# A hybrid decoder layer in one launch: the output projection by seven half products for two tiles, in one block with the gates, and the first expert weights requested later

## The chip, the core and the metric

The kernel is one program on one core of a Trainium2 chip. The metric is the device time of one execution in microseconds. All matmuls are float32 and each appears in the trace as two matmul records, so that a count of records is twice the count of matmuls in the code.

## What is computed

One inference step of one decoder layer, for 512 prompt tokens and 32 new tokens (8 sequences of 4), which travel together as 544 columns. The parts that matter here are the end of the mixer and the mixture of experts:

```
merged = g_a * (y_a @ w_out_ssm) + g_b * (y_b @ w_out_att) + g_c * (y_c @ w_out_sc)   # gates: sigmoid
x = x + gate1 * (merged @ w_o)                      # w_o: 1024 x 1024, the output projection
h = rms_norm(x, norm2_w) * (1 + scale2) + shift2
x = x + gate2 * hier_moe(h)                         # 32 experts, two for each token
# hier_moe: router logits, top group, top 2 in it, then for each expert
# silu(h @ w_gate[e]) * (h @ w_up[e]) @ w_down[e]   # 1024 x 256, 1024 x 256, 256 x 1024
```

## The kernel before, in words

The activations lie transposed: 128 partitions, 8 chunks of features, 544 columns, and `HALF` is 272 columns. A weight tile is 128 output features by 1024 input features (512 KB). SP loads such tiles in one long order into a ring of 8 buffers. Semaphore `w_used` counts the tiles that TensorE has finished with, and the load of tile n waits for it to reach n - 7.

**The gates (end of the block that begins before L1460).** Eight steps, w = 0 to 7, each take two weight tiles. Put as a 2 x 2 block product (two output tiles, two halves of the input features, two halves of the columns) a pair of tiles is eight products of four matmuls each (`half_product`, L362), and the kernel makes it with seven: VectorE forms four sums of weight halves (`weight_sum`, L383) and four sums of activation blocks (`act_sums`), and puts the seven results together from PSUM (`block_step`, L388 to L401). Results wait in 8 PSUM banks in turn. After each second step VectorE multiplies by the gate and adds into `merged` (L2024, L2025).

**The output projection (a block of its own, L2120 to L2149 and on).** A block starts when all five engines have met at a barrier. TensorE takes the eight tiles of `w_o`, numbers `T_O` to `T_O` + 7, one after the other with `project` (L350): 16 matmuls of 128 x 128 by 272 columns for a tile. VectorE adds each tile, times gate1, to `xT` (L2145 to L2148) and counts `s_res`. SP loads `xT` again at the block's start (L2123). ScalarE squares and scales each finished chunk of x, GpSimd adds the squares, and TensorE begins the router's logits (L2204) when seven chunks are done.

**The experts (same block).** The 32 experts are handled as 16 pairs. For each pair SP loads the gate and up weights (two DMAs of 2048 KB, L2366, three buffers) and the down weights come in two DMAs of 1024 KB (pairs 0 and 1 from SP at L2371, the others from ScalarE's queue at L2503, two buffers). The rows of h are written to DRAM (`h2_rows`, from ScalarE's queue, L2189), and GpSimd gathers the rows of a pair from there with an indirect DMA (L2403) and scatters the results (L2411). TensorE turns the gathered rows (L2426), makes gate and up (L2440), then the down product of the pair before (L2461). What orders SP's queue is written out by hand:

```
with sp.Fori(0, trips) as r:
    gate_up_in(r, 0)
    down_in(r, 0)
    down_in(r, 1)
    sp.wait_ge(w_used, T_END)
    gate_up_in(r, 1)
    sp.wait_ge(s_slot, 1)
    ...
    sp.wait_ge(gath[0], r * (8 * NP) + 16)
    for p in range(2, NP):
        gate_up_in(r, p)
```

So pairs 0 and 1 are requested before the first gathered rows have landed, and pair 2 only after they have. Pair 3 waits until the gate and up product of pair 0 has freed its buffer, and so on.

## Time and profile before

| | |
|---|---|
| median of 3 runs | 1494.41 us (1492.55 to 1501.58) |
| the profiled execution, its own time | 1493.89 us |
| its span in the trace | 1492.2 us |
| TensorE busy | 1357.6 us, 91% of the span |
| VectorE, ScalarE, GpSimd busy | 44%, 17%, 9% |
| output projection, first to last matmul | 1111.9 to 1173.6 us |
| first expert matmuls to the end of the last pair | 1198.6 to 1448 us |
| read from HBM over the span | 234.47 MB |

The span is the stretch that the trace covers; 1.7 us of the execution's own time lie around it. The shares are means over stages with different limits, so that the stages are read one by one below. "PEclk" is the clock that TensorE was granted as a share of 2.4 GHz, and 0.50 is its lower level, 1.2 GHz.

### The profile page before, as it was taken

To read this page: it belongs to the slowest core of one execution; us is meant where nothing else is said; L and a number is where in the kernel's file an instruction comes from. 1 tells how busy PE (TensorE), PEld (TensorE's weight loads), DVE (VectorE), ACT (ScalarE), POOL (GpSimd) and SP (SyncE) were. 2 spreads that over 40 slices of the span, in tenths; PEclk is the share of its full clock that TensorE was granted. 3 is DMA by queue.
4 is the path that set the end of the run, shared out by engine and by line. 5 is a ranking of instruction groups with operands and counts; after the bars stand their busy time and mean duration, and the time that the engine had idled before them with its cause. 6 is when DMAs were issued, how large, how long until landed. Compare 5 with 4: busy or idle time off the path is not lost. (4 is left out here: it accounts for less than half of the span.)

```text
span 1492.2 us, 19377 instructions
## 1 busy us (share of the span) xinstructions
PE 1357.6 (91%) x7089; PEld 977.8 (66%) x7089; DVE 662.2 (44%) x1371; ACT 257.7 (17%) x554; POOL 139.5 (9%) x270
## 2 busy tenths in 40 slices
PE   4999999999999999899989988899989888878784
PEld 2787677878778788576767766688878633222233
DVE  1635677555667756110115557575541412111125
ACT  2201211221223521110112122310001300000001
POOL 0223000000000000122210002000001111111111
PEclk9999999999999999899999997999999989999995
DMA  8463323322322223556461102321245489999945
GB/s 343 166 135 107 101 63 113 124 84 91 113 85 91 99 77 111 167 163 205 163 237 43 43 29 88 143 63 65 85 151 220 173 340 425 425 424 425 409 157 180
DMA packets 62208, 250.87 MB, mean 168 GB/s; under 512 B 10058, under 2 KB 20714, under 8 KB 53002
## 3 DMA queue, kind: packets, MB, share of 16 engines
q1 hardware_dynamic: 42130, 185.31, 34.0%
q10 hardware_dynamic: 10264, 44.97, 8.4%
q0 software_dynamic: 9728, 19.42, 3.9%
q8 instruction: 57, 0.93, 0.3%
q14 instruction: 29, 0.24, 0.1%
HBM read 234.47 MB, written 22.91 MB: 172 GB/s over the span
## 5 line engine op out<-in xcount | busy, mean ns | idle before, releaser
L350 PE MATMUL psum<-arena 128*128 128x272 f32 x2048 | 488.2, 397 | 10.4 <-DVE arena L1997 4.8
L350 PEld LDWEIGHTS psum<-arena 128*128 128x128 f32 x2048 | 391.2, 192 | 103.3 <-issue 16.3
L362 PE MATMUL psum<-arena 128*128 128x272 f32 x840 | 197.3, 394 | 0.0
L362 PEld LDWEIGHTS psum<-arena 128*128 128x128 f32 x840 | 157.6, 189 | 39.8 <-issue 6.7
L1203 PE MATMUL psum<-arena 128*128 128x272 f32 x512 | 124.4, 401 | 0.0
L2440 PE MATMUL psum<-arena 128*64 128x512 f32 x512 | 115.2, 601 | 2.7 <-DVE arena L2539 2.7
L1203 PEld LDWEIGHTS psum<-arena 128*128 128x128 f32 x512 | 97.3, 193 | 26.1 <-DVE arena L1334 4.1
L2440 PEld LDWEIGHTS psum<-arena 128*64 128x64 f32 x512 | 35.8, 136 | 70.9 <-issue 70.9
L2461 PE MATMUL psum<-arena 128*64 128x512 f32 x256 | 69.3, 690 | 1.2 <-DVE arena L2528 1.2
L1334 DVE TENSOR_TENSOR arena<-arena,psum 128x272 f32<-128x272 f32 x16 | 7.0, 439 | 140.2 <-ACT arena L1286 140.2
L1522 PE MATMUL psum<-arena 128*128 128x272 f32 x256 | 64.7, 407 | 2.9 <-PEq L206 2.9
L1039 DVE MATCH_REPLACE8 arena<-arena 32x1056 f32<-32x1056 f32 (+3 forms) x80 | 64.9, 817 | 0.0
L1036 DVE MAX8 arena<-arena 32x8 f32<-32x1056 f32 (+3 forms) x80 | 63.4, 825 | 0.9 <-DVE arena L727 0.3
L1017 DVE SCALAR_TENSOR_TENSOR arena<-psum,arena 128x128 f32<-128x128 f32 (+3 forms) x32 | 15.7, 491 | 99.8 <-PE psum L840 99.8
L1522 PEld LDWEIGHTS psum<-arena 128*128 128x128 f32 x256 | 49.8, 199 | 13.7 <-issue 3.1
L2426 PE MATMUL psum<-arena 128*128 128x128 f32 x128 | 22.5, 333 | 37.2 <-DMA arena<-h_rows,arena 37.1
L2520 DVE TENSOR_TENSOR arena<-arena,psum 128x256 f32<-128x256 f32 x16 | 6.8, 422 | 108.0 <-ACT arena L2509 108.0
L2426 PEld LDWEIGHTS psum<-arena 128*128 128x128 f32 x128 | 17.6, 169 | 50.3 <-DMA arena<-h_rows,arena 45.7
L2461 PEld LDWEIGHTS psum<-arena 128*64 128x64 f32 x256 | 19.8, 158 | 40.9 <-issue 39.5
L572 POOL DMA_DIRECT2D arena<-in_pages_i x64 | 33.3, 521 | 118.5 <-issue 112.2
L2528 DVE TENSOR_SCALAR arena<-psum,arena 128x1024 f32<-128x1024 f32 x16 | 20.6, 1284 | 51.1 <-PE psum L2461 51.1
L335 PE MATMUL psum<-arena 128*32 128x512 f32 x192 | 24.8, 636 | 19.9 <-DMA arena<-in_weights 19.9
(374 smaller groups left out, 1414.9 us busy)
## 6 DMA issues: line engine op xcount, KB each, us to landing
arena<-in_weights SPq DMA_DIRECT2D x153, 512.0 KB, 4.4
arena<-in_w_gu SPq DMA_DIRECT2D x32, 2048.0 KB, 17.5
arena<-in_w_down ACTq DMA_DIRECT2D x28, 1024.0 KB, 17.1
arena<-in_weights ACTq DMA_DIRECT2D x16, 512.0 KB, 4.2
arena<-in_x SPq DMA_DIRECT2D x2, 2176.0 KB, 10.7
arena<-in_pages_k POOLq DMA_DIRECT2D x32, 128.0 KB, 3.2
arena<-in_pages_k SPq DMA_DIRECT2D x32, 128.0 KB, 2.6
arena<-in_pages_v SPq DMA_DIRECT2D x32, 128.0 KB, 2.9
```

The source lines that it names most:

```text
L335: mm = pe.matmul(psum[32 * j:32 * j + 32, bank, :], lhsT=c_silu[:, 2 * j + c2, :], rhs=ring[:, (first + j) % RING, c2 * 512:c2 * 512 + 512 ...
L350: mm = pe.matmul(out[:, h, :], lhsT=w_of(n, c), rhs=act[:, c, h * HALF:(h + 1) * HALF], start=(c == 0), stop=(c == DC - 1))
L362: mm = pe.matmul(out, lhsT=w[:, c * P:c * P + P], rhs=x[:, c, :], start=(c == 0), stop=(c == 3))
L572: pool.dma_start(kidx[64 * a:64 * a + 64, bass.ds(b, 1), j * PAGE:(j + 1) * PAGE].rearrange("p a n -> p (a n)"), ins["pages_i"][bass.ds(of ...
L1036: dve.max(best8[0:s.shape[0], i, :], s).then_inc(s_top, 1)
L1039: dve.match_replace(s, best8[0:s.shape[0], i, :], s, CHOSEN).then_inc(s_top, 1)
L1203: mm = pe.matmul(psum[:, bank, 0:HALF], lhsT=w_of(n, c), rhs=act_of[:, c, h * HALF:(h + 1) * HALF], start=(c == 0), stop=(c == DC - 1))
L1522: mm = pe.matmul(psum[:, (2, 7)[k % 2], 0:HALF], lhsT=w_of(n, c), rhs=act_of[:, c, (k % 2) * HALF:(k % 2 + 1) * HALF], start=(c == 0), sto ...
L2426: mm = pe.transpose(psum[:, c // 4, (c % 4) * P:(c % 4) * P + P], xg[:, p % 2, c * P:c * P + P], const("ident"))
L2440: mm = pe.matmul(psum[CAP * e:CAP * e + CAP, 2 + k, :].rearrange("p (o f) -> p o f", o=2), lhsT=xgT[:, k, at:at + CAP], rhs=wv[:, c], star ...
L2461: mm = pe.matmul(psum[CAP * e:CAP * e + CAP, 4 + h, :], lhsT=actT[:, k, at:at + CAP], rhs=w_dn[k][:, e, f * D + h * 512:f * D + h * 512 + ...
L2528: dve.tensor_scalar(yst[:, k, :].rearrange("p (a n) -> p a n", n=512), psum[:, 4:6, :], wtab[:, p:p + 1], None, ALU.mult).then_inc(s_yo, 1)
```

## The change

The projection is made like the gates: two tiles at a time (v = 0 to 3), seven half products each. It stands in the gates' block now, with no barrier between. The halves of a pair's two tiles are taken in swapped order (`SWAPPED`), so that the tile with the lower number is finished first, at step k = 5, and the other at k = 6. The weight sums of a pair are formed during the pair before, those of v = 0 in the gates' last step. The sums of the activations, `t_m`, lie where the first expert buffer `a_q` is, so SP requests no expert weights before `s_res` has reached 8; and `s_gu`, which the first request waits for too, is raised by TensorE only at `T_END`.

```diff
+        SWAPPED = (1, 0)
+        t_m = [A.at(a_q + 4 * HALF * i, 4, HALF) for i in range(4)]
...
-                        if w + 1 < N_SEVEN:
-                            weight_sum(dve, n + 2, wsum[:, (w + 1) % 2], k, sum_link)
+                        weight_sum(dve, n + 2, wsum[:, (w + 1) % 2], k, sum_link, SWAPPED if w + 1 == N_SEVEN else (0, 1))
...
+                    dve.wait_ge(s_mgw, w // 2 + 1)
+                    if w == 3:
+                        act_link(dve.tensor_tensor(t_m[0], block_of(merged, 0, 1), block_of(merged, 0, 0), ALU.subtract))
...
-        with nc.Block() as block:
             @block.sync
             def _(sp):
                 sp.dma_start(xT, ins["x"]).then_inc(s_x10, 16)
 
             @block.tensor
             def _(pe):
-                pe.sem_inc(s_gu, 2)
-                pe.sem_inc(s_dn, 2)
-                for u in range(8):
-                    tile_ready(pe, T_O + u)
-                    if u >= 4:
-                        pe.wait_ge(s_res, u - 3)
-                    project(pe, T_O + u, pair[u % 4], merged).then_inc(w_used, 1)
+                for v in range(4):
+                    n = T_O + 2 * v
+                    for k, (wv, x) in enumerate(seven_operands(n, sums_o[v], merged, t_m, SWAPPED)):
+                        j = 7 * v + k
+                        if k == 0:
+                            tile_ready(pe, n + 1)
+                            pe.wait_ge(s_mgw, 2)
+                        if j == 1:
+                            pe.wait_ge(s_mgw, 4)
+                        if k == 2:
+                            pe.wait_ge(s_wsum, 4 * (N_SEVEN + v) + 2)
+                            pe.wait_ge(s_asum, 10)
+                        if k == 3:
+                            pe.wait_ge(s_wsum, 4 * (N_SEVEN + v) + 3)
+                            pe.wait_ge(s_asum, 11)
+                        if k == 4:
+                            tile_ready(pe, n)
+                            pe.wait_ge(s_asum, 12)
+                        if k == 6:
+                            pe.wait_ge(s_wsum, 4 * (N_SEVEN + v) + 4)
+                        pe.wait_ge(s_took, 53 + j if j < 4 else max(56, 49 + j))
+                        mm = half_product(pe, psum[:, (j + 4) % 8, 0:HALF], wv, x)
...
+                    if v == 1:
+                        pe.wait_ge(w_used, T_O + 2)
+                        pe.sem_inc(s_dn, 2)
+                pe.wait_ge(w_used, T_END)
+                pe.sem_inc(s_gu, 2)
...
+                def residual(m, src):
+                    gate, dst, new = mods[:, 16 + m, :], xT[:, m, 0:SEQ], xT[:, m, SEQ:NT]
+                    dve.scalar_tensor_tensor(dst, src[:, 0:SEQ], gate[:, 0:1], dst, ALU.mult, ALU.add)
...
+                        block_step(dve, k, psum[:, (7 * v + k + 4) % 8, 0:HALF], (part8[:, 0, :], part8[:, 1, :]),
+                                   blocks_of(tmw), took)
+                        for i in {2: (0, 1), 3: (2,), 5: (3,)}.get(k, ()):
+                            if v < 3:
+                                weight_sum(dve, n + 2, sums_o[v + 1], i, sum_link, SWAPPED)
+                        if k >= 5:
+                            if v == 0 and k == 5:
+                                dve.wait_ge(s_x10, 16)
+                            residual(2 * v + k - 5, tmw[:, 6 - k, :])
...
                 with sp.Fori(0, trips) as r:
+                    sp.wait_ge(s_res, DC)
                     gate_up_in(r, 0)
                     down_in(r, 0)
```

What this does to the order of instructions is shown at three places. The names of waits there are those under which a semaphore was first allocated; many are used again under other names.

TensorE before, from the last half product of the gates into the projection's first two tiles (L1460 and L2125 are the end and the start of the blocks; `qk_ready` stands for the weight sums):

```order
L362 MATMUL psum<-arena 128x272 [waits dve_link3,qk_ready]
L362 MATMUL psum<-arena 128x272 x3
L1460 UNCONDITIONAL_BRANCH
L2125 UNCONDITIONAL_BRANCH [waits barrier_Pool_Activation_PE_DVE_SP_release]
L350 MATMUL psum<-arena 128x272 [waits w_full1]
L350 MATMUL psum<-arena 128x272 x15
L350 MATMUL psum<-arena 128x272 [waits w_full2]
L350 MATMUL psum<-arena 128x272 x15
```

The same place now (`exp_ready` is `s_mgw`, the merged tiles; `logits_read` is `s_asum`, the sums of activations; `dve_link3` is `s_took`):

```order
L362 MATMUL psum<-arena 128x272 [waits dve_link3,qk_ready]
L362 MATMUL psum<-arena 128x272 x3
L2132 UNCONDITIONAL_BRANCH
L362 MATMUL psum<-arena 128x272 [waits dve_link3,exp_ready,w_full2]
L362 MATMUL psum<-arena 128x272 x3
L362 MATMUL psum<-arena 128x272 [waits dve_link3,exp_ready]
L362 MATMUL psum<-arena 128x272 x3
L362 MATMUL psum<-arena 128x272 [waits dve_link3,logits_read,qk_ready]
L362 MATMUL psum<-arena 128x272 x3
L362 MATMUL psum<-arena 128x272 [waits dve_link3,logits_read,qk_ready]
L362 MATMUL psum<-arena 128x272 x3
```

The barrier is gone from between the two stages, and two tiles take 7 x 4 matmuls where they took 2 x 16.

VectorE before, the last tile of the projection (L2145 waits for TensorE's last matmul of it):

```order
L2145 SCALAR_TENSOR_TENSOR arena<-psum,arena 128x272 [waits rel_in_dram,w_used]
L2145 SCALAR_TENSOR_TENSOR arena<-psum,arena 128x240
L2146 TENSOR_TENSOR arena<-psum,arena 128x32
L2148 TENSOR_TENSOR arena<-arena 128x32 [waits rel_in_dram]
L2150 TENSOR_SCALAR arena<-arena 128x512 [waits rel_in_dram]
```

VectorE now, from the sixth product of the last pair to the same L2150 (L2198 now); `top_step` counts the half products:

```order
L398 TENSOR_TENSOR arena<-arena,psum 128x272 [waits top_step,dve_link3]
L399 TENSOR_TENSOR arena<-arena,psum 128x272
L2173 SCALAR_TENSOR_TENSOR arena<-arena 128x512 [waits dve_link3]
L2174 TENSOR_TENSOR arena<-arena 128x32
L2175 TENSOR_TENSOR arena<-arena 128x32 [waits rel_in_dram]
L401 TENSOR_TENSOR arena<-arena,psum 128x272 [waits rel_in_dram,w_used]
L2173 SCALAR_TENSOR_TENSOR arena<-arena 128x512 [waits dve_link3]
L2174 TENSOR_TENSOR arena<-arena 128x32
L2175 TENSOR_TENSOR arena<-arena 128x32 [waits rel_in_dram]
L2198 TENSOR_SCALAR arena<-arena 128x512 [waits rel_in_dram]
```

Chunk 6 is finished between the last two products, and one step of the seven stands ahead of chunk 7.

SP before, from the last ring load to the last request ahead of pair 2:

```order
L308 DMA arena<-in_weights 128x1024 [waits w_used]
L1460 UNCONDITIONAL_BRANCH
L2121 UNCONDITIONAL_BRANCH [waits barrier_Pool_Activation_PE_DVE_SP_release]
L2123 DMA arena<-in_x 128x4352
...
L2366 DMA arena<-in_w_gu 128x4096 [waits sturned_out]
L2366 DMA arena<-in_w_gu 128x4096
...
L2371 DMA arena<-in_w_down 128x2048 [waits short_in_psum]
...
L2366 DMA arena<-in_w_gu 128x4096 [waits sturned_out,w_used]
L2366 DMA arena<-in_w_gu 128x4096
```

SP now (`modulation_turned` is `s_res`):

```order
L308 DMA arena<-in_weights 128x1024 [waits w_used]
L2128 UNCONDITIONAL_BRANCH
L2130 DMA arena<-in_x 128x4352
...
L2414 ISA [waits modulation_turned]
L2416 DMA arena<-in_w_gu 128x4096 [waits satt_out]
L2416 DMA arena<-in_w_gu 128x4096
...
L2421 DMA arena<-in_w_down 128x2048 [waits short_gate]
...
L2416 DMA arena<-in_w_gu 128x4096 [waits satt_out,w_used]
L2416 DMA arena<-in_w_gu 128x4096
```

The order of SP's queue is the same; the load of x has lost the barrier ahead of it, and the first request of expert weights has gained the wait for all eight residuals.

## Rows read from the trace of the kernel before

**Rows 1.** Windows: us, busy time by engine (records), PEclk, DMA share, GB/s.

```profile
1173.50:1190.00 16.50, 13.54 (x128) 9.64 (x127) 11.48 (x67) 6.91 (x9) 1.35 (x2) 1.00 0.94 360
1190.00:1198.50 8.50, 4.33 (x80) 3.94 (x80) 2.90 (x18) 3.03 (x5) 2.13 (x2) 0.62 0.39 120
1198.50:1230.00 31.50, 28.74 (x130) 11.84 (x132) 5.80 (x6) 1.54 (x4) 4.03 (x4) 0.89 0.94 374
1230.00:1400.00 170.00, 137.40 (x600) 49.65 (x596) 29.74 (x31) 8.07 (x21) 20.18 (x20) 0.91 1.01 424
```

**Rows 2.** Waits from 1190 us on: who for whom, total us, times, longest.

```profile
PE psum L2426 <- DMA arena<-h_rows,arena: 37.1, 12, 4.4
```

**Rows 3.** Timeline from the last gates to the projection: start, us, engine, line.

```profile
1085.68 22.23 PE L362 MATMUL psum<-arena 128*128 128x272 f32 x96
...
1094.13 0.69 DVE L383 TENSOR_TENSOR arena<-arena 128x512 f32<-128x512 f32 x1
...
1108.01 0.44 DVE L401 TENSOR_TENSOR arena<-arena,psum 128x272 f32<-128x272 f32 x1 [1.05 <-PE psum L362]
1108.48 1.29 DVE L2024 TENSOR_TENSOR arena<-arena 128x1088 f32<-128x1088 f32 x1
...
1109.81 1.29 DVE L2025 TENSOR_TENSOR arena<-arena 128x1088 f32<-128x1088 f32 x1
1111.59 0.35 SPq L2123 DMA_DIRECT2D arena<-in_x  x1
...
1111.94 61.63 PE L350 MATMUL psum<-arena 128*128 128x272 f32 x256 [4.03 <-PEq L1460]
```

**Rows 4.** Windows of the projection's first 8 us, columns as above.

```profile
1112.00:1116.00 4.00, 4.00 (x9) 3.07 (x10) 0.00 (x0) 1.09 (x2) 1.66 (x1) 0.50 0.97 311
1116.00:1120.00 4.00, 4.00 (x17) 3.20 (x17) 0.00 (x0) 0.00 (x0) 0.00 (x0) 0.89 1.03 443
```

**Rows 5.** Timeline: VectorE takes tiles 1 and 2 of the projection.

```profile
1129.39 0.88 DVE L2145 SCALAR_TENSOR_TENSOR arena<-psum,arena 128x272 f32<-128x272 f32 x2 [6.10 <-PE psum L350]
...
1136.76 0.88 DVE L2145 SCALAR_TENSOR_TENSOR arena<-psum,arena 128x272 f32<-128x272 f32 x2 [6.17 <-PE psum L350]
```

**Rows 6.** Timeline at the end of the projection.

```profile
1173.50 3.22 PE L2204 MATMUL psum<-arena 128*36 128x256 f32 x28
1173.60 25.70 SPq L2366 DMA_DIRECT2D arena<-in_w_gu  x4
1173.61 0.88 DVE L2145 SCALAR_TENSOR_TENSOR arena<-psum,arena 128x272 f32<-128x272 f32 x2 [6.17 <-PE psum L350]
...
1174.61 0.19 DVE L2148 TENSOR_TENSOR arena<-arena 128x32 f32<-128x32 f32 x1
```

**Rows 7.** DMA requests from 1112 to 1132 us: count, size of each, us to landing.

```profile
arena<-in_w_gu SPq DMA_DIRECT2D x2, 2048.0 KB, 15.4
arena<-in_w_down SPq DMA_DIRECT2D x4, 1024.0 KB, 22.5
```

**Rows 8.** DMA requests from 1173 to 1198 us, columns as above.

```profile
h_rows<-arena ACTq DMA_DIRECT2D x4, 512.0 KB, 6.5
h_rows<-arena ACTq DMA_DIRECT2D x1, 128.0 KB, 2.9
arena<-h_rows,arena POOLq DMA_INDIRECT x2, 3.9
```

**Rows 9.** Landing of L2123's load of x (all of the run).

```profile
DMA to landing us min/median/max: 8.8/8.8/8.8
```

**Rows 10.** Landing of L2403's third gather, requested at 1201.37.

```profile
DMA to landing us min/median/max: 11.3/11.3/11.3
```

**Rows 11.** Timeline of the experts: the first gather, and TensorE after two waits.

```profile
1194.36 1.12 POOL L2403 DMA_INDIRECT arena<-h_rows,arena  x1 [12.48 <-issue]
...
1248.45 1.97 PE L2426 MATMUL psum<-arena 128*128 128x128 f32 x8 [3.93 <-DMA arena<-h_rows,arena]
...
1415.24 1.09 PE L2426 MATMUL psum<-arena 128*128 128x128 f32 x8 [2.43 <-DMA arena<-h_rows,arena]
```

More of the change, by code:

```diff
@@ L369, in act_sums, with tile_halves, weight_sum @@
                 link(dve.tensor_tensor(out, a, b, ALU.subtract))
-        def tile_halves(n):
-            return [ring[:, (n + i) % RING, 512 * k:512 * k + 512] for i in range(2) for k in range(2)]
-        def weight_sum(dve, n, sums, k, link):
-            a11, a12, a21, a22 = tile_halves(n)
+        def tile_halves(n, order=(0, 1)):
+            return [ring[:, (n + i) % RING, 512 * k:512 * k + 512] for i in order for k in range(2)]
+        def weight_sum(dve, n, sums, k, link, order=(0, 1)):
+            a11, a12, a21, a22 = tile_halves(n, order)
             if k == 0:
@@ new lines, in build @@
+            s_h2w = [sem(f"h2_written{i}") for i in range(4)]
+            acc11 = A.at(a_e + 2048, NT)
+            sq11 = A.at(a_e + 2048 + NT, 4, NT)
+            a_r11 = a_w + 8 * D
+            std11 = A.at(a_r11, P)
+            std_new = A.at(a_r11 + P, NEW)
+            lgT = A.at(a_r11 + 160, 256)
+            lgT_new = A.at(a_r11 + 416, NEW, parts=36)
+            rcol = A.at(a_r11 + 448, 5)
+            dshift = A.at(a_r11 + 456, DC, NB)
+            a_r = a_r11 + NT
+            NR = 5
@@ new lines, in build @@
+            W_LG = NE + 8
+            lg = A.at(a_r, NR, W_LG)
+            g8, e8 = A.at(a_r + 220, NR, 8), A.at(a_r + 260, NR, 8)
+            gi8, ei8 = A.at(a_r + 300, NR, 8), A.at(a_r + 340, NR, 8)
+            gif, eif = A.at(a_r + 380, NR, 1), A.at(a_r + 385, NR, 2)
+            goh = A.at(a_r + 395, NR, NG)
+            gexp = A.at(a_r + 415, NR, NG)
+            gsum = A.at(a_r + 435, NR)
+            masked = A.at(a_r + 440, NR, NE)
+            pen = A.at(a_r + 600, NR, NG)
+            full = [A.at(a_r + 720 + 160 * k, NR, NE) for k in range(2)]
@@ new lines, in build @@
+            wcol = A.at(a_param + PARAM_AT["conv_prev"][0], 2, NR)
+            a_keep = a_param + PARAM_AT["conv_prev"][0] + 16
+            rounds_i = A.at(a_keep + 20, 1).bitcast(I32)
+            rows11 = A.at(a_xb + DC * NT - 2 * D, 4, D)
+            assert T_O % RING + 3 < RING and T_END - T_O == RING
+            sums_o = [wsum[:, 0], A.at(a_xb + DC * NT, 4, 512)] + [
+                A.at(a_ring + (T_O + 2 * v) % RING * 1024, 4, 512) for v in range(2)]
+            h2_rows = nc.dram_tensor("h2_rows", [NT, D], F32).ap()
@@ L2148, in _ @@
                     link(dve.tensor_tensor(new, new, tmp, ALU.add))
                     dve.sem_inc(s_res, 1)
+                for out, a, b in ((t_m[1], block_of(merged, 1, 1), t_m[0]),
+                                  (t_m[2], block_of(merged, 1, 1), block_of(merged, 0, 1)),
+                                  (t_m[3], block_of(merged, 1, 0), t_m[1])):
+                    act_link(dve.tensor_tensor(out, a, b, ALU.subtract))
+                for v in range(4):
+                    n = T_O + 2 * v
+                    for k in range(7):
+                        if k < 6:
+                            dve.wait_ge(s_prod, 6 * (N_SEVEN + v) + k + 1)
+                        else:
+                            dve.wait_ge(w_used, n + 2)
+                        block_step(dve, k, psum[:, (7 * v + k + 4) % 8, 0:HALF], (part8[:, 0, :], part8[:, 1, :]),
[7 more added lines that the diff above has]
+                            residual(2 * v + k - 5, tmw[:, 6 - k, :])
```

169 lines of the change are left out of this document (70 added, 99 removed).

## The prediction

> **What bounds the kernel now.** I read the windows of busy time first, since they tell which resource is full in which stage. In the projection TensorE never pauses once it has begun: 61.63 us for 256 matmul records [rows 3]. In the router and the row writing no single resource is full, and a chain through all engines sets the time; the DMA engines move 360 GB/s in its first part and 120 in its last 8.5 us [rows 1]. From 1230 to 1400 us the DMA share is 1.01 at 424 GB/s while TensorE works 137 of 170 us [rows 1]: the experts run at the speed of the weight stream. The list of waits says the same from TensorE's side: it waits 12 times, 37.1 us in all, for gathered rows [rows 2], which travel in that full stream. The last of these waits ends at 1415.24 [rows 11]; from there TensorE works from pair to pair. So the reader should keep two clocks apart: when TensorE is done with the projection, and when the DMA engines have moved what the gather behind 1415.24 has ahead of it. All times below are in the profiled execution (span 1492.2, own time 1493.89, 0.5 under the median of the runs).
>
> **The projection, part by part.**
>
> Matmuls: 96 records of half products took 22.23 us, eight records to a product, so 12 products, 1.85 us each [rows 3]. Four tile pairs take 28 products where they took 32: 4 x 1.85 = 7.4 us less.
>
> The barrier: TensorE ended the gates at 1107.91 and began the projection at 1111.94, 4.03 us later [rows 3]. Now product 0 needs only merged tiles 0 to 3, long ready, and runs at once, to 1109.8. Product 1 needs `merged` complete: VectorE's L401, L2024 and L2025 end at 1109.81 + 1.29 = 1111.1 [rows 3]. I take 1111.2, so 1.4 us of idleness are left and 2.6 us go. Behind it the sums t_m[1] to t_m[3] cost 1.29 each, like L2025; they are ready by 1112.5, 1113.8 and 1115.1, and products 2, 3 and 4 want them at 1113.0, 1114.9 and 1116.7. The margin is 0.5 us at the narrowest.
>
> The clock: after the 4.03 us of idleness TensorE was granted 0.50 (1.2 GHz) for the next 4 us and 0.89 on average in the 4 after [rows 4]. A tile at full clock took 1136.76 - 1129.39 = 7.37 us [rows 5], eight would be 59.0, and 61.63 were spent: 2.7 us of loss. An idle time of 2.43 us was followed by eight records in 1.09 us, one of 3.93 us by the same eight in 1.97 us [rows 11], so I take it that 1.4 us leave the clock at its upper level. Bounds: 0 and 2.7 us.
>
> TensorE then ends at 1111.2 + 27 x 1.85 = 1161.2 instead of 1173.57 [rows 3], 12.4 us earlier.
>
> What hides the rest: VectorE has in 7 x 1.85 = 13.0 us eight steps of 0.44 (L401), four weight sums of 0.69 (L383) [rows 3] and two residuals of about 1.1, together 8.5 us. Without that cover each us of excess would be paid four times. The load of x, 8.8 us from request to landing [rows 9], is now requested once the products of the gates are done, some 2.5 us before the 1111.59 of today [rows 3]; it lands by 1118 and is wanted after product 5, at 1120.4.
>
> The tail: today the eighth residual is done 1.2 us after TensorE (1174.8 against 1173.57) [rows 6]. Now the sixth product's two steps (0.8) and residual 6 (about 1.1) fill VectorE to about TensorE's end + 0.1, then one step (0.44) and residual 7 (1.1): done at + 1.7, or 1162.9. TensorE's first logits want the seventh residual, at + 0.2 instead of at once (L2204) [rows 6], and those of the last chunks have the whole row of 28 matmul records ahead of them: 0.3 us of the gain goes back. The router would thus be 12 us early.
>
> **The weights, part by part.** Before, pairs 0 and 1's down weights and pair 0's gate and up weights came during the projection: 2 x 2048 + 4 x 1024 KB = 8.4 MB [rows 7], when the DMA engines had nothing else. Only pair 1's gate and up followed at 1173.60 [rows 6]. Now all four sets, 12.6 MB, start at 1162.9. At 424 GB/s the 8.4 MB that are moved cost 19.8 us of a resource that is full later. Three stretches have room for them, each read as its length x (1 - rate / 424) [rows 1]: 16.5 us at 360 give 2.5, 8.5 us at 120 give 6.1, 31.5 us at 374 give 3.7. Together 12.3 us.
>
> The stream ended its critical part at 1415.2, 241.6 us after the request at 1173.60. The same now: 1162.9 + 241.6 - 12.3 + 19.8 = 1412.0, if every gap is filled. Two will not be: about 1 us from a request to its first bytes, and about 1 us where pair 3 must wait for pair 0's gate and up product (both are estimates; the gaps themselves are inside the 12.3). That makes 1414.0 and a change of **-1.2 us**. The bounds of this term are -3.2 us (all gaps filled) and the case below in which the gaps come back.
>
> The sum needs the first gather to land before the queue of weights runs dry, since pair 2 is requested only then. Queue and row writes hold 12.6 + 2.2 MB = 35 us, to about 1198.8. The gather was requested 20.8 us after TensorE's end (1194.36) [rows 11]. With 0.3 us of tail, and the last row write slower than its 2.9 us [rows 8] by some 2.5 us (the large ones took 6.5 beside a weight load [rows 8]), that is 1184.8. A gather beside a weight load took 11.3 us [rows 10], against 3.9 in a quiet stretch [rows 8]: landing at 1196.1, before the queue is dry, and 2 to 3 us before today's 1198.5. After 1415 nothing changes.
>
> A rule of the Trainium skill speaks to the last step. The third gather, requested into a running weight load, took 11.3 us, but had to wait until about that load's end [rows 10]; this alone doesn't tell whether it was served side by side or after. "DMA: Bandwidth & Descriptors", under Queues, rings and completion order, says that each of the 16 engines goes round between its queues packet by packet. By that rule the gather is served side by side at any depth of the queue, and the sum is the one above; without it, it would be the second rival's.
>
> **Rivals.**
>
> *The lead arrives whole.* If the experts were paced by the gather's delay and not by bytes, everything would shift by 12.4 - 0.3 = 12.1 us: 1481.8. For it: TensorE waits for rows and not for weights [rows 2]. Against it: the DMA share of 1.01 for 170 us [rows 1]; a delay with free bandwidth would show less. Half of it could still come through if the 424 GB/s can be exceeded a little. Chance 0.08.
>
> *The gather starves, and it ends slower.* If rows are served only when the weights queued ahead are done, the first gather lands as much after the dry queue as the third did after its load: two transfers, 4.2 MB or 9.9 us, requested at 1198.5 and under way 1 us later, end at 1209.4; the gather landed at 1201.37 + 11.3 = 1212.7 [rows 10], 3.3 us after. So it lands at 1198.8 + 3.3 = 1202.1 where it landed at 1198.5. Nothing overlaps, pair 2 is requested 3.6 us late, and the time is 1497.5. It decides from the point where the landing is later than 1198.5, that is, when the gather takes over 14 us. Slower row writes ahead of it could add some 3 us. For it: gathers deep in the stream take much longer than 11.3. Against it: those compete with two queues more. Chance 0.22.
>
> *The clock stays down after the 1.4 us.* TensorE ends 2.7 us later, every request too: +1.5 us, 1495.4. Chance 0.1.
>
> *The half products don't do what they say:* if a sum or a bank came late once in each pair of tiles, by 1 to 2 us, the lead would shrink by 4 to 8 us, and through the stream's start all of it would show: 1497 to 1501. The margin of 0.5 us above is the only thin one and occurs once, so 0.05.
>
> **How the numbers follow.** My forecast, 0.55, is -1.2 us: **1492.7 us**, with its own range from 1490.5 to 1495. The range of 8 in 10 reaches to the starving gather above, 1499, and part of the way to the whole lead below, 1486. A measurement of this kernel can't tell a change under about 1% (15 us) from none. None of the cases leaves that band; what does must be something that I don't see. Slower gets a little more, 0.06, since a bubble in the stream would repeat with each pair; faster 0.03; within 1% 0.91.
>
> **What would show it.** In the profile of the changed kernel: one idle time of 1.4 us on TensorE before the second projection product, at full clock after it; 28 products in about 52 us, ending near 1161; the eighth residual near 1163, with the weight requests right behind it; the DMA share full from there through the router, where it now sinks to 0.39; the first gather taking 8 to 14 us, landing near 1196; the last wait of TensorE for rows ending at about 1414. The prediction is wrong if the DMA share shows holes before 1230, if the gather lands after 1200, or if the experts' stretch from first to last matmul shrinks below today's.

## The result, and the profile after

Before, the median of 20 runs was 1496.92 us; after, also of 20, it was 1503.76 us (1498.65 to 1507.88). The ratio is 1.0047, with a 95% interval of 1.0036 to 1.0058: 7.0 us slower (5.4 to 8.7), where 1.2 us faster was forecast with a range that ended at 1499. One of the 20 runs before took 3171.76 us, twice as long as the others, and the ratio leaves it out.

The profiled execution (span 1505.2, own time 1506.99) has 6.4 of its extra microseconds before the change begins: the gates' last product ends at 1114.35 instead of 1107.91, with the same instructions ahead of it. The other kernels below, with that same code ahead, reach this point between 1107.3 and 1111.1, so I take this part for scatter from run to run; the medians of the 20 runs bear this out, as they differ by 6.8 us and not by the 13 of the two spans. I therefore count all times from two marks: **G**, the end of the gates' last product, and **E**, the end of TensorE's work for the projection. The third mark, **D**, is the start of the last down product (16 records of 128x512).

The timeline of the changed kernel around the projection and the router (start, us, engine and line, operation, tiles, count, then idle time before it and who ended it), with the first row write, and then where the experts begin and end:

```profile
1116.24 1.29 DVE L2026 TENSOR_TENSOR arena<-arena 128x1088 f32<-128x1088 f32 x1
1117.59 49.91 PE L362 MATMUL psum<-arena 128*128 128x272 f32 x216 [1.42 <-DVE arena L2026]
...
1117.78 3.95 DVE L2181 TENSOR_TENSOR arena<-arena 128x1088 f32<-128x1088 f32 x3 [0.25 <-DVE arena L2026]
...
1167.80 3.22 PE L2253 MATMUL psum<-arena 128*36 128x256 f32 x28 [0.30 <-DVEq L2176]
...
1170.70 0.82 SPq L2416 DMA_DIRECT2D arena<-in_w_gu  x2
...
1171.65 2.06 SPq L2421 DMA_DIRECT2D arena<-in_w_down  x4
...
1173.82 0.93 SPq L2416 DMA_DIRECT2D arena<-in_w_gu  x2
...
1176.45 0.34 ACTq L2238 DMA_DIRECT2D h_rows<-arena  x1
...
1186.37 1.01 ACT L2236 ACTIVATE arena<-psum 32x1024 f32<-32x1024 f32 x1 [5.35 <-DMA h_rows<-arena]
1187.41 0.34 ACTq L2238 DMA_DIRECT2D h_rows<-arena  x1
...
1200.03 1.12 POOL L2454 DMA_INDIRECT arena<-h_rows,arena  x1 [23.85 <-issue]
...
1210.40 0.82 SPq L2416 DMA_DIRECT2D arena<-in_w_gu  x2
1210.51 1.97 PE L2477 MATMUL psum<-arena 128*128 128x128 f32 x8 [17.07 <-DMA arena<-h_rows,arena]
...
1457.68 3.65 PE L2512 MATMUL psum<-arena 128*64 128x512 f32 x16 [1.20 <-DVE arena L2579]
```

The first row write, the first turning and D in the kernel before:

```profile
1182.14 0.34 ACTq L2189 DMA_DIRECT2D h_rows<-arena  x1
...
1198.59 1.97 PE L2426 MATMUL psum<-arena 128*128 128x128 f32 x8 [2.06 <-DMA arena<-h_rows,arena]
...
1444.46 3.65 PE L2461 MATMUL psum<-arena 128*64 128x512 f32 x16 [1.20 <-DVE arena L2528]
```

The first half is what the change promised. The 4.03 us in front of the projection [rows 3] have become 1.42; 216 records in 49.91 us follow without a pause; E is 1117.59 + 49.91 = 1167.50. From G that is 53.15 us, against 65.66 before: TensorE has a lead of **12.5 us**. The lead is gone when TensorE turns its first gathered rows. Before, that was at 1198.59, 25.0 us after E. Now it is at 1210.51, 43.0 us after E: 18.0 us more. 18.0 - 12.5 = 5.5 us late, and D - G has grown by 6.8 us (1457.68 - 1114.35 = 343.3; before 1444.46 - 1107.91 = 336.6). TensorE's wait for the rows was 17.07 us long, where it had been 2.06.

Why the rows are late stands in the DMA requests from 1160 to 1210 us (count, size of each, median us to landing), to be held against [rows 8]:

```profile
h_rows<-arena ACTq DMA_DIRECT2D x4, 512.0 KB, 13.3
h_rows<-arena ACTq DMA_DIRECT2D x1, 128.0 KB, 11.4
arena<-h_rows,arena POOLq DMA_INDIRECT x2, 10.4
```

The gather took 10.4 us; 11.3 had been forecast. But it was requested 32.5 us after E instead of 20.8, as it waits for all five row writes. The four large ones took 13.3 us instead of 6.5 in the median, and the small last one 11.4 instead of 2.9. ScalarE had to wait 5.35 us for the first write before it could prepare the last. How the two streams share the DMA engines is seen in the queues' packets (packets, MB, share): in the changed kernel from 1190 to 1195, with q1 carrying weights and q10 the row writes,

```profile
q1 hardware_dynamic: 197, 1.39, 66.3%
q10 hardware_dynamic: 196, 0.74, 36.0%
```

and in the kernel before from 1187 to 1191, when the weights of pair 1 are in and only rows are left:

```profile
q10 hardware_dynamic: 430, 1.55, 94.7%
q1 hardware_dynamic: 1, 0.00, 0.0%
```

One packet of the one, one of the other: beside weights the row writes get 0.74 MB in 5 us, or 150 GB/s, and alone 390. This is the rule of the Trainium skill that the prediction weighed ("DMA: Bandwidth & Descriptors", Queues, rings and completion order: each engine goes round between its queues packet by packet), and the trace agrees. I had applied it to the gather and not to the writes ahead of it.

The windows after (us, busy time by engine with records, PEclk, DMA share, GB/s) answer to [rows 1]:

```profile
1178.00:1203.00 25.00, 9.41 (x108) 8.06 (x108) 8.09 (x44) 6.13 (x7) 2.13 (x2) 0.63 1.01 419
1203.00:1211.00 8.00, 0.49 (x3) 0.49 (x4) 0.00 (x0) 0.00 (x0) 0.00 (x0) 0.50 0.77 323
1211.00:1230.00 19.00, 16.33 (x69) 6.89 (x70) 2.87 (x3) 0.77 (x2) 2.00 (x2) 0.80 0.90 346
1230.00:1400.00 170.00, 140.49 (x616) 50.72 (x613) 30.96 (x32) 8.07 (x21) 20.20 (x20) 0.91 1.01 423
```

The router's stretch is full now (1.01), as forecast. But the queue runs dry before the gather lands (the DMA share is 0.97 from 1206 to 1209 and 0.17 from 1209 to 1211), and the gap comes back as 0.77 and 0.90 until pair 2, requested at 1210.40, fills it.

### The profile page after: what moved, and what is told of

Read it like the earlier page. It is cut to its first block and busy times, and to the rows that moved or that the text cites. A ratio compares the mean times of both kernels' runs of the same rounds, so it can differ in the third digit from the quotient of the medians.

```text
span 1505.2 us, 19389 instructions
## 1 busy us (share of the span) xinstructions
PE 1355.8 (90%) x7057; PEld 976.3 (65%) x7057; DVE 695.8 (46%) x1415; ACT 257.7 (17%) x554; POOL 141.8 (9%) x270
## 5 line engine op out<-in xcount | busy, mean ns | idle before, releaser
L350 PE MATMUL psum<-arena 128*128 128x272 f32 x1792 | 426.3, 396 | 5.8 <-DVE arena L1998 4.8
L350 PEld LDWEIGHTS psum<-arena 128*128 128x128 f32 x1792 | 340.9, 191 | 87.0 <-issue 11.9
L362 PE MATMUL psum<-arena 128*128 128x272 f32 x1064 | 249.1, 393 | 1.4 <-DVE arena L2026 1.4
L362 PEld LDWEIGHTS psum<-arena 128*128 128x128 f32 x1064 | 199.9, 189 | 50.6 <-issue 6.7
L1203 PE MATMUL psum<-arena 128*128 128x272 f32 x512 | 125.3, 403 | 0.0
L1203 PEld LDWEIGHTS psum<-arena 128*128 128x128 f32 x512 | 98.0, 194 | 26.7 <-DVE arena L1334 4.1
L1524 PE MATMUL psum<-arena 128*128 128x272 f32 x256 | 64.8, 407 | 2.9 <-PEq L206 2.9
L1039 DVE MATCH_REPLACE8 arena<-arena 32x1056 f32<-32x1056 f32 (+3 forms) x80 | 64.9, 817 | 0.0
L2477 PEld LDWEIGHTS psum<-arena 128*128 128x128 f32 x128 | 17.4, 168 | 65.8 <-DMA arena<-h_rows,arena 46.2
L1524 PEld LDWEIGHTS psum<-arena 128*128 128x128 f32 x256 | 49.8, 199 | 13.6 <-issue 3.1
L383 DVE TENSOR_TENSOR arena<-arena 128x512 f32<-128x512 f32 x76 | 52.7, 693 | 2.6
L2590 DVE TENSOR_TENSOR arena<-psum,arena 128x1024 f32<-128x1024 f32 x16 | 19.6, 1225 | 61.9 <-PE psum L2477 61.9
L2512 PEld LDWEIGHTS psum<-arena 128*64 128x64 f32 x256 | 19.8, 159 | 41.2 <-issue 39.8
## 6 DMA issues: line engine op xcount, KB each, us to landing
arena<-in_x SPq DMA_DIRECT2D x2, 2176.0 KB, 11.7
```

The lines of the kernel that those rows point to most:

```text
L350: mm = pe.matmul(out[:, h, :], lhsT=w_of(n, c), rhs=act[:, c, h * HALF:(h + 1) * HALF], start=(c == 0), stop=(c == DC - 1))
L362: mm = pe.matmul(out, lhsT=w[:, c * P:c * P + P], rhs=x[:, c, :], start=(c == 0), stop=(c == 3))
L383: link(dve.tensor_tensor(sums[:, k], a, b, op))
L1039: dve.match_replace(s, best8[0:s.shape[0], i, :], s, CHOSEN).then_inc(s_top, 1)
L1203: mm = pe.matmul(psum[:, bank, 0:HALF], lhsT=w_of(n, c), rhs=act_of[:, c, h * HALF:(h + 1) * HALF], start=(c == 0), stop=(c == DC - 1))
L1524: mm = pe.matmul(psum[:, (2, 7)[k % 2], 0:HALF], lhsT=w_of(n, c), rhs=act_of[:, c, (k % 2) * HALF:(k % 2 + 1) * HALF], start=(c == 0), sto ...
```

## The experiments

Two explanations were tested. **The writes** (theory 1, "turns", in what was expected of the runs): the late request for weights makes the row writes slow, so the gather is late, and everything behind the first turning follows it at a fixed distance. **The bytes** (theory 2): 8.4 MB moved out of an idle stretch cost their time in a full one, whatever the gather does. Below each run is told with D - G against the 336.6 us of before, which is free of the scatter ahead of G.

**before_late.** The old projection with only the weights asked for later.

```diff
                 with sp.Fori(0, trips) as r:
+                    sp.wait_ge(s_res, DC)
                     gate_up_in(r, 0)
```

> The kernel before, with one line more: SP waits for all eight residuals before the first request of expert weights; projection, barrier and all else as before. E is the end of TensorE's last projection matmul; in the kernel before the first gathered rows land at E + 24.9 and TensorE's last wait for rows ends at E + 241.7, in the changed one at E + 42.9 and E + 260.8. Theory 1 (turns): the DMA engines take the queues in turn, packet by packet, so the row writes crawl as long as weights are queued; the first gather's landing comes late, and the end follows it by 217 us. Then this kernel shows the delay alone: landing near E + 41, last wait near E + 258.5, +17 us against before. Theory 2 (bytes): only the 8.4 MB that now fall into the busy stretch count, less the gaps that they fill: +9.5 us, landing near E + 33.

Measured: ratio 1.0091 (1.0070 to 1.0113), +13.6 us. D - G is 353.4, or +16.8. The timeline shows the same crawl without the new projection:

```profile
1204.72 1.12 POOL L2404 DMA_INDIRECT arena<-h_rows,arena  x1 [23.55 <-issue]
...
1214.26 1.97 PE L2427 MATMUL psum<-arena 128*128 128x128 f32 x8 [16.77 <-DMA arena<-h_rows,arena]
```

The large writes took 12.3 us, the last one 12.0, and the first turning came 41.4 us after E. The +16.8 and the landing are those of the writes; the bytes alone would have given +9.5, which lies below the interval of the ratio (10.5 to 16.9 us). So the late request alone costs 14 us, and the new projection beside it gives back 13.6 - 7.0 = 6.6 us (10.0 by D - G).

**down_first.** The change, but with the down weights of pairs 0 and 1 asked for as early as before. Of the 8.4 MB, only pair 0's gate and up weights (4.2 MB) stay late.

```diff
                 with sp.Fori(0, trips) as r:
-                    sp.wait_ge(s_res, DC)
-                    gate_up_in(r, 0)
                     down_in(r, 0)
                     down_in(r, 1)
+                    sp.wait_ge(s_res, DC)
+                    gate_up_in(r, 0)
```

> The changed kernel with SP's first requests in another order: the down weights of pairs 0 and 1 (4.2 MB) as soon as the first pair of projection tiles is done, only then the wait for the eight residuals and the gate and up weights of pairs 0 and 1. Theory 1 (turns): behind 8.4 MB instead of 12.6 the weights run dry at about E + 26, the row writes end at about E + 28, the first gather lands at about E + 32.5 instead of E + 42.9, and the end moves by the same 10 us: 10 us faster than the changed kernel, 3 to 4 faster than before. Theory 2 (bytes): 4.2 MB less in the full stretch is worth 9.9 us only if the gaps stay filled; the landing moves little. A third, that the hole in the DMA share after 1205 us is what costs: the hole stays, since pair 2 is still requested at the landing, and the gain is under 5 us.

Measured: 0.9996 (0.9978 to 1.0013). The first turning is 37.6 us after E, D - G +2.3. I had expected the writes to be freed sooner and the rows to land near E + 32.5: the large ones took 16.6 us, longer than in the change. The queues from 1174 to 1179 show why:

```profile
q1 hardware_dynamic: 119, 1.69, 79.1%
q10 hardware_dynamic: 117, 0.44, 21.4%
```

Again one packet for one. But a packet of weights here has 1.69 MB / 119 = 14 KB in the mean, where it had 7 KB in the changed kernel from 1190 to 1195, and a packet of rows 3.8 KB. The sizes stand in the packet records: gate and up weights travel in packets of 16384 bytes, down weights in 8192 and rows in 4096, each the run of one partition, with some of 4 bytes between them that lower the means. So the writes get 88 GB/s: what a small transfer gets beside a large one depended here on the packets of the large one.

**quiet.** The change with no expert weights at all until the first gather has landed.

```diff
                 with sp.Fori(0, trips) as r:
+                    sp.wait_ge(gath[0], r * (8 * NP) + 16)
                     sp.wait_ge(s_res, DC)
```

> The changed kernel with no expert weights requested at all until the first gathered rows have landed, so that the row writes and the first gather run with nothing beside them. Theory 1 (turns): the row writes take about 3 us each instead of 9.8 to 16.5, the last one under 3 instead of 11.4, the gather about 3.9; landing at E + 23 to E + 25, as the router's chain alone allows. All 12.6 MB and pair 2 then come after it: 29.7 us of stream where 9.9 stood before, so the last wait is near E + 24 + 217 + 18 = E + 259, about the same as the changed kernel (within 4 us). Theory 2 (bytes): the router's chain and the landing hardly depend on the weights (over E + 35), and the end is 15 us later than the changed kernel's.

Measured: 1.0131 (1.0107 to 1.0156), +19.6 us; D - G +17.6. The writes took 2.6 and 2.0 us, and the first turning came 25.8 us after E, 17 us sooner than in the change. Then TensorE stands for weights:

```profile
1188.32 1.96 PE L2478 MATMUL psum<-arena 128*128 128x128 f32 x8 [1.45 <-DMA arena<-h_rows,arena]
...
1202.33 9.37 PE L2492 MATMUL psum<-arena 128*64 128x512 f32 x32 [12.05 <-DMA arena<-in_w_gu]
...
1223.01 9.27 PE L2492 MATMUL psum<-arena 128*64 128x512 f32 x32 [9.92 <-DMA arena<-in_w_gu]
```

This shows both: without weights beside them the writes are fast, and the bytes are a cost of their own once the rows are early. My forecast of its end was too low: I had counted 18 us of stream still to come behind the rows, and the stretch from the first turning to D grew by 28 us over the changed kernel's (275.3 against 247.2). For this kernel's time the bytes account, 15 us over the changed kernel, was the nearer one (12.6 by the ratios).

**split_writes.** The change with the second and fourth row write issued by GpSimd, so that the writes stand in two queues and should get two turns of three.

```diff
+                    if i in (1, 3):
+                        return
                     act.wait_ge(s_row_sb, i + 1)
...
+                for i in (1, 3):
+                    pool.wait_ge(s_row_sb, i + 1)
+                    pool.dma_start(h2_rows[i * P:i * P + P, :], rows11[:, i, :]).then_inc(s_h2w[i], 16)
```

> The changed kernel with the writes of row blocks 1 and 3 issued from GpSimd's queue instead of ScalarE's; the requests of weights stay as changed. Theory 1 (turns): two queues of row packets get two turns for each turn of the weights; the writes end near E + 23 instead of E + 32, the first gather lands near E + 34, and the time falls by about 8 us against the changed kernel. Theory 2 (bytes) and any account in which a queue's number does not count: no change within 2 us.

Measured: 1.0020 (1.0003 to 1.0037), +3.0 us; D - G +2.8. The gather was requested 28.0 us after E instead of 32.5, and the first turning came at +38.8 instead of +43.0. The 4 us of earlier rows came back as 4 us of time. It was half of the 8 us that I had expected, as the last write (5.5 us) still has to wait for the first, which took 11.2 (1169.78 to 1181.00). The queues from 1180 to 1184, with q0 carrying GpSimd's writes, show the two turns of three:

```profile
q1 hardware_dynamic: 118, 0.84, 49.9%
q10 hardware_dynamic: 114, 0.45, 27.6%
q0 software_dynamic: 118, 0.42, 25.6%
```

**hold_pair1** and **hold_gather.** Down weights first as in down_first; pair 1's and pair 2's gate and up weights asked for only when the row writes have landed, or when the first gather has. The cuts show SP's waits; the moved `down_in` is as above.

```diff
                     sp.wait_ge(w_used, T_END)
+                    for k, n in enumerate((2, 1, 1, 1)):
+                        sp.wait_ge(s_h2w[k], 16 * n)
                     gate_up_in(r, 1)
...
-                    sp.wait_ge(gath[0], r * (8 * NP) + 16)
```

```diff
                     sp.wait_ge(w_used, T_END)
+                    sp.wait_ge(gath[0], r * (8 * NP) + 16)
                     gate_up_in(r, 1)
...
-                    sp.wait_ge(gath[0], r * (8 * NP) + 16)
```

> The changed kernel with the down weights of pairs 0 and 1 requested after the first tile pair, pair 0's gate and up weights after the eight residuals, and pair 1's and 2's only when the row writes have landed. E is TensorE's end of the projection; the mark of the end is the last turning of gathered rows (E + 253.8 before, E + 273.1 in the changed kernel), which so far came 229 to 231 us after the first gather's landing. Turns: the row writes meet one load of 4.2 MB as they did before, the gather is requested near E + 21, then shares turns with pair 1's weights (11 us) and lands near E + 32.5; the mark is near E + 262.5 and the time 10 us under the changed kernel's, 3 to 4 under before. Bytes only: same or 5 us better than down_first, with the landing near E + 37.

> Like the kernel with pair 1 held, but pair 1's and 2's weights wait for the first gathered rows themselves. Turns: the gather runs alone (4 us) and lands near E + 25; 4.2 MB more than before are then still to come, 9.9 us less the 1 to 2 of gaps that they fill, so the mark is near E + 262.5, as with the other. If the landing alone sets the end, whatever is still to be loaded, the mark is near E + 255 and the time 10 us under before.

Measured: hold_pair1 0.9995 (0.9981 to 1.0010), hold_gather 0.9990 (0.9975 to 1.0006). The last write took 2.9 us in both, but the large ones 8.9 and 9.2, and the first turning was at +34.7 and +28.1, 2 to 3 us behind what was expected. Against the kernel before neither can be told from no change, where I had expected 3 to 4 us less. D - G is -2.2 and +0.3: in hold_gather the rows are earlier by 6.6 us, but the 4.2 MB of pair 1 are still to come and take the gain, as in quiet.

**pair2_early.** The change with pair 2 asked for when the row writes have landed, not the gather. It was meant to fill the gap of 0.77.

```diff
-                    sp.wait_ge(gath[0], r * (8 * NP) + 16)
+                    for k, n in enumerate((2, 1, 1, 1)):
+                        sp.wait_ge(s_h2w[k], 16 * n)
```

> The changed kernel with one wait changed: pair 2's weights are requested when the row writes have landed, not when the gathered rows have. It fills the hole in the DMA share between 1203 and 1211 us. If the end follows the landing (pair 3's request waits for pair 0's product, which waits for the rows), the gain is 2 us at most: mark at E + 271 to E + 273. If the hole is what costs, as much as it is long, the mark is near E + 267 and the time 5 us or more under the changed kernel's.

Measured: 1.0059 (1.0039 to 1.0079); D - G +6.5, the change's own 6.8 within its scatter. The first turning was at +43.5. The gap of 0.77 is gone, but it comes back behind the turning. The windows at the same distance from the turning as those of 0.77 and 0.90:

```profile
1197.70:1205.70 8.00, 0.51 (x3) 0.51 (x4) 0.00 (x0) 0.00 (x0) 0.00 (x0) 0.50 1.01 428
1205.70:1224.70 19.00, 16.34 (x69) 6.81 (x69) 2.87 (x3) 0.77 (x2) 1.99 (x2) 0.81 0.75 295
```

Pair 3's request waits for pair 0's product, which waits for the rows. It is made 13.0 us after the turning in the changed kernel (first row) and 12.7 us after it here (second row):

```profile
1223.47 0.83 SPq L2416 DMA_DIRECT2D arena<-in_w_gu  x2
...
1217.91 0.82 SPq L2416 DMA_DIRECT2D arena<-in_w_gu  x2
```

So this run moved the bubble in the stream, which I had named as what would make the prediction wrong, and did not remove it. It shows that requesting pair 2 earlier is worth nothing while pair 3 hangs on the rows; what a stream without the bubble would give it doesn't show.

**barrier_back.** The change with the projection in a block of its own again.

```diff
+        with nc.Block() as block:
             @block.sync
```

> The changed kernel with the projection in a block of its own again, so that the barrier stands ahead of its first product; products, sums and requests as changed. TensorE is idle for 4 us or a little more instead of 1.4, and its clock falls to 0.50 for some 4 us: E comes 4 to 5.5 us later after the end of the gates. What follows is counted from E and doesn't change, so the time is 4 to 5.5 us over the changed kernel's.

Measured: 1.0088 (1.0068 to 1.0109), 0.41% or 6 us slower than the change, where 4 to 5.5 were expected. TensorE's row:

```profile
1114.41 53.40 PE L362 MATMUL psum<-arena 128*128 128x272 f32 x224 [3.89 <-PEq L1462]
```

After 3.89 us of idleness 224 records take 53.40 us. At 1.85 us for eight, the pace of the 216 above, they would take 51.8; 1.6 us are the clock, whose granted value was 0.58 in the mean from 1114 to 1118. G to E is 57.3 us against 53.15, or 4.1 more. D - G grows by 4.4 over the change. What TensorE loses in front of the projection is lost one for one.

**gu0_early.** The version that the above points to. Tiles and partial products are moved in memory so that pair 0's gate and up weights find their place free before the projection, and come during it, with pair 0's down weights. Only pair 1's gate and up weights are asked for at the end of the projection, and its down weights later still, behind pair 2's gate and up.

```diff
-        t_m = [A.at(a_q + 4 * HALF * i, 4, HALF) for i in range(4)]
+        t_m = [A.at(a, 4, HALF) for a in (a_q + 8192, a_sc + 2048, a_sc + 2048 + 2 * NT, a_sc + 2048 + 4 * NT)]
...
-                    sp.wait_ge(s_res, DC)
+                    sp.wait_ge(s_mgw, 4)
                     gate_up_in(r, 0)
                     down_in(r, 0)
-                    down_in(r, 1)
                     sp.wait_ge(w_used, T_END)
...
                         gate_up_in(r, p)
+                        if p == 2:
+                            down_in(r, 1)
```

> The changed kernel with its sums and partial results of the projection moved out of the first expert buffer (sums of activations to the place that pair 1's down weights take later and to the row buffer, partial results to the row and result buffers, whose clearing by GpSimd moves behind the eighth residual), so that pair 0's gate and up weights are requested when the gates are done and its down weights after the first tile pair, both during the projection; pair 1's gate and up weights are requested at TensorE's end, as before, and pair 1's down weights with pair 2's, after the first gathered rows. E is TensorE's end of the projection. Turns: the row writes and the gather meet what they met before, so the rows land near E + 25 to E + 26; the last down product starts 246 to 248 us after that where nothing is left to load, here 3 to 4 us more for the 2.1 MB of down weights: E + 275, against E + 270.9 before and E + 290.2 in the changed kernel. With E 12.5 us earlier the time is 8 us under before (0.5 per cent) and 15 us under the changed kernel. If instead the shorter projection couldn't give its lead through the expert stream at all, the time would be that of before, within 1.5 us, as in the three kernels with late weights.

Measured: **0.9959 (0.9940 to 0.9978)**, median 1491.20 against 1496.20, or 6.1 us less by the ratio (3.3 to 9.0), where 8 were expected. D - G is -5.7. In its timeline the weights start at 1110.84, and the gather is requested 21.8 us after E:

```profile
1110.84 0.82 SPq L2420 DMA_DIRECT2D arena<-in_w_gu  x2
...
1182.48 1.24 POOL L2459 DMA_INDIRECT arena<-h_rows,arena  x1 [12.67 <-issue]
...
1186.77 1.97 PE L2482 MATMUL psum<-arena 128*128 128x128 f32 x8 [1.31 <-DMA arena<-h_rows,arena]
```

The row writes took 5.4 and 2.8 us, and the first turning was at +26.1, nearly as early as in the kernel before. Half of the lead of 12.5 us arrives. Of the other 6.8 us, 1.1 are lost before the turning (26.1 against 25.0) and 5.7 behind it (turned to D is 251.6 us, 245.9 before), where 2.1 MB of pair 1's down weights are still to come, 5 us at 424 GB/s; that these are the cause fits, but no run takes them away by themselves. The windows there are full at once, and TensorE hardly pauses:

```profile
1200.00:1210.00 10.00, 8.84 (x48) 4.07 (x46) 1.92 (x3) 0.84 (x3) 1.00 (x1) 1.00 1.03 432
1210.00:1230.00 20.00, 20.00 (x97) 6.91 (x97) 5.59 (x6) 1.15 (x3) 3.65 (x4) 1.00 1.01 424
```

**All of them together** (us; "turned" is TensorE's first turning of gathered rows; the measured change is the ratio less 1, times 1497; D - G is of one execution, and lies within 3.2 us of it):

| kernel | G to E | E to turned | turned to D | change of D - G | measured change |
|---|---|---|---|---|---|
| before | 65.7 | 25.0 | 245.9 | | |
| after | 53.2 | 43.0 | 247.2 | +6.8 | +7.0 |
| before_late | 64.9 | 41.4 | 247.1 | +16.8 | +13.6 |
| down_first | 53.2 | 37.6 | 248.2 | +2.3 | -0.6 |
| split_writes | 53.2 | 38.8 | 247.4 | +2.8 | +3.0 |
| hold_pair1 | 53.2 | 34.7 | 246.5 | -2.2 | -0.7 |
| pair2_early | 53.2 | 43.5 | 246.4 | +6.5 | +8.8 |
| barrier_back | 57.3 | 43.0 | 247.4 | +11.1 | +13.2 |
| gu0_early | 53.2 | 26.1 | 251.6 | -5.7 | -6.1 |
| hold_gather | 53.2 | 28.1 | 255.6 | +0.3 | -1.5 |
| quiet | 53.2 | 25.8 | 275.3 | +17.6 | +19.6 |

In the first eight rows turned to D hardly moves (245.9 to 248.2), though the turning moves by 18 us and the bytes asked for late by 8.4 MB. In the same eight, pair 3's gate and up weights are requested 11.9 to 13.3 us after the turning, and D comes 233.5 to 235.9 us after that request. In the last three, weights of pairs 0 and 1 are outstanding when the rows arrive: 2.1, 4.2 and 12.6 MB.

## Why the prediction was wrong

**The lead at TensorE: right.** Four products fewer, 1.42 us of idleness (1.4 forecast), and the clock at its upper level after it. The window from 1116 to 1120 reads 1.00, where [rows 4] had 0.50 and 0.89:

```profile
1116.00:1120.00 4.00, 2.58 (x12) 2.01 (x12) 3.68 (x4) 0.00 (x0) 0.46 (x1) 1.00 0.95 365
```

G to E was 53.15 us, 53.3 forecast. The three sums behind the first, 3.95 us, never held up TensorE. Two rivals are out by these rows: that the clock stays down, and that half products come late.

**The tail: 1.3 us short.** The eighth residual was done 3.0 us after E (1170.33 + 0.19), not 1.7. The term that was too small is residual 7 at about 1.1 us; it took 2.2 (from 1168.30) and holds a VectorE instruction that took 1.33 us instead of 0.19, as the last section tells. It delays the request for weights (1170.70). The first row write was asked for at 1176.45, 8.95 us after E, and before at 1182.14, 8.57 after: 0.4 us of the lead go here, 0.3 forecast.

**The gather itself: right.** 10.4 us, 11.3 forecast, beside a queue that was full until 1.4 us before it landed. The 10.4 us alone don't rule out the rival by which rows are served only when the weights ahead are done, since the gather did land just after those. The packets from 1205 to 1207, with q0 carrying the gather, do:

```profile
q1 hardware_dynamic: 39, 0.64, 74.6%
q0 software_dynamic: 40, 0.16, 19.9%
```

Here too it is one for one. Yet this rival came closest, with a landing at E + 40.9 (1202.1 - 1161.2) against the measured E + 42.9, 1497.5 us, and "slower row writes ahead of it could add some 3 us". It was right about the landing by another mechanism: the writes were held up, and the gather only through them. The rival of late half products has 1497 to 1501 too, under a condition that did not occur.

**The step that failed** is "the last row write slower than its 2.9 us [rows 8] by some 2.5 us". It was slower by 8.5 us, and the four large ones, whose 6.5 us I carried over, by 6.8 us in the median. I took 6.5 us as the price of a write beside a weight load. In [rows 8] the load ended while the writes were running: the queues before, from 1187 to 1191, hold one packet of weights to 430 of rows. By the rule that I cited for the gather, each packet of a write waits for one of the weights; I didn't work out what that makes of a write with weights beside it to the end. So the gather was requested 32.5 us after E instead of the 23.6 forecast (1184.8 - 1161.2). Against before (20.8) these are 11.7 us more: 0.4 of tail, 2.9 since the first write came back after 9.9 us instead of 7.0 and ScalarE needs its place for the last one, and 8.4 in the last write itself. The 8.9 us over the forecast, less the 0.9 that the gather was faster, put the landing 8.0 us too late, and that is the miss of 8.2 within its scatter. The runs bear it out: split_writes takes 4 us off the writes and the time falls by 4, quiet makes them fast, and before_late makes them slow in the old kernel. Two of the prediction's own signs of being wrong came with it: the gather landed after 1200, at 1210.4 or E + 42.9, and the DMA share has a hole before 1230. For the size, the table gives D - G = 53.2 + 43.0 + 247.2, of which only the middle term was unforeseen. The clock is no rival for the 7 us: after the 17.07 us of waiting TensorE ran at 0.80 in the mean from 1211 to 1230, but what this costs lies in turned to D, which grew by 1.3 us.

**The sum over bytes was the wrong account, though it can bind.** Taking 19.8 us for 8.4 MB and 12.3 us back for the gaps treats the stream from E to the last wait as one that runs whenever it has room. It doesn't: pair 3 is requested some 13 us after the turning, whatever has come in before. pair2_early fills a gap ahead of the turning and gets one behind it, and before_late moves the same bytes with turned to D within 1.2 us of before. The distance from the first turning to D is about 247 us as long as the weights of the first two pairs are in by then; the bytes bind when they aren't (quiet, hold_gather, half of gu0_early's lead). About 13 us of it lie ahead of pair 3's request; behind it the DMA share is 1.01 from 1230 on, which fits a full stream that is set going by that request. Whether the bytes or TensorE keep the remaining 234 us is not settled by these runs. The rival by which the lead arrives whole assumed pacing by the gather: the pacing is there, but the lead was spent ahead of it.

The prediction also held that no change under 15 us can be told from none; here the interval of 5.4 to 8.7 us tells 7 us from none.

**What would have made it right.** hold_pair1 has its first turning at E + 34.7, the forecast's own 34.9 (1196.1 - 1161.2), and a change of -0.7 us, between -2.8 and +1.5; the forecast was -1.2. That the sum over bytes gives about this number for such a landing is luck, as its account is wrong; what the run supports is that the landing decided.

## What to carry to other kernels

Before moving a large load, list the small transfers on the critical path that will now run beside it to their end, and price each by its share of packets there, not by a duration from a stretch where the load ended in between. A lead won on the busiest engine is worth only what is left of it at the next thing that all later work waits for; find that point and check what moves into the time ahead of it. Here the same arithmetic saving is worth -0.41% when the weights come early and +0.47% when they come late.

## What the hardware showed that I had not expected

**Packets, not bytes, were shared out.** 197 to 196 and 119 to 117 packets, with mean sizes of 7 or 14 KB against 3.8; and 118 to 114 to 118 with three queues. The same 512 KB write took 2.6 us alone (quiet), 6.5 where the weights ran out while the four were under way (before), 13.3 beside weights (after) and 16.6 beside the larger packets (down_first). A part of it passes before the first packet: 0.9 us from the request of the first write to its first packet in quiet (1171.52 to 1172.37), but 3.4 beside weights (after, 1176.45 to 1179.90) and 3.3 in the kernel before (1182.14 to 1185.44).

**VectorE and GpSimd hold each other up.** In the changed kernel's timeline at the end of the projection:

```profile
1159.21 1.34 POOL L2394 TENSOR_TENSOR arena<-arena 128x544 f32<-128x544 f32 x1 [1.10 <-ACT arena L2213]
...
1167.26 0.19 DVE L2174 TENSOR_TENSOR arena<-arena 128x32 f32<-128x32 f32 x1
...
1168.30 0.75 DVE L2173 SCALAR_TENSOR_TENSOR arena<-arena 128x512 f32<-128x512 f32 x1
...
1168.50 1.75 POOL L2394 TENSOR_TENSOR arena<-arena 128x544 f32<-128x544 f32 x1 [7.95 <-ACT arena L2213]
1168.97 1.33 DVE L2174 TENSOR_TENSOR arena<-arena 128x32 f32<-128x32 f32 x1
1170.33 0.19 DVE L2175 TENSOR_TENSOR arena<-arena 128x32 f32<-128x32 f32 x1
```

An addition of 128x32 takes 0.19 us, and 1.33 when GpSimd's addition is running: it ends at 1170.30, just after GpSimd's at 1170.25. Of the eight L2174 of the projection three fall beside such an addition and take 1.33 us, the five others 0.19. GpSimd's takes 1.34 us alone and 1.75 when it starts under VectorE's L2173. The Trainium skill has the rule ("SBUF — State Buffer", Who interferes with whom): a VectorE instruction with two inputs in SBUF and a GpSimd instruction that reads SBUF share a read interface, and whichever starts first keeps it to its end. The trace agrees.
